# A state-space scan turned to channels on partitions, inside a fused decoder block

## The chip, the core and the metric

One core of a Trainium2 chip runs the whole block as one program. The metric is the device time of one execution in microseconds; the median of several runs counts. TensorE (PE) multiplies, VectorE (DVE), ScalarE (ACT) and GpSimd (POOL) do the elementwise work, and SyncE (SP) issues nearly all transfers.

## What is computed

One decoder layer on 512 positions of width 1024, in float32. The part that the change touches is the third mixer, a chunked state-space scan with 8 heads of 64 channels, 2 groups and a state of 128, in 4 chunks of 128 positions:

```python
xd = xh * dt[..., None]                                   # (chunk, 128, head, 64)
cs = cumsum(dt * a)                                       # within a chunk
scores = einsum("bclhn,bcshn->bclsh", ch, bh) * exp(cs_l - cs_s, lower triangle)
y_diag = einsum("bclsh,bcshp->bclhp", scores, xd)
states = einsum("bclhn,bclh,bclhp->bchpn", bh, exp(cs_end - cs), xd)
# prev: the states, carried from chunk to chunk with exp(cs_end)
y_off = einsum("bclhn,bchpn,bclh->bclhp", ch, prev, exp(cs))
y = y_diag + y_off + d_skip[:, None] * xh
y = rms_norm(y.reshape(bsz, s_len, 512) * silu(z), ssm_norm_g)
x = x + concatenate([u, att, y], axis=-1) @ w_out
```

Ahead of it stand the norm of x, the combined projection `h @ w_in` (z, x/B/C and dt are columns of it) and a causal convolution of 4 taps. Two more mixers (a convolution module and a sparse attention) fill the other columns; a second norm and a feed-forward part with 2816 hidden channels follow.

## The kernel before

The program is one list of steps, `PLAN`, built by `make_plan` (line 104). Every engine walks through the same list and does its own share of each step, so the order of the list is the order of work on each engine, and semaphores tie the engines together. The list is made of 92 slots. Each slot begins with a step `("mg", c, q)`: a quarter of the projection with weight chunk `c`, 12 matmuls of 512 columns on TensorE. A weight is split into two float32r parts (`w_hi` by ACT, line 927, `w_lo` by DVE, line 639), and so is what it is multiplied with; three products stand for one (`product`, line 1747). The other steps are placed in the slots by hand, before (`front`) or behind (`fill`) the slot's own. Chunks of weights come in this order: convolution, indexer, q, k, v, convolution, x/B/C, z, and from slot 68 on `out` for attention, convolution and scan (two halves of four slots each), then the feed-forward part in loops.

PSUM has 8 banks, in three rings that `make_groups` (line 259) lays out: `acc` (4 banks, projections), `aux` (3 banks, small products) and `out` (one bank, `pv` and `yd`). Each small product takes the next bank of its ring, and `claim` makes TensorE wait until that bank was emptied.

The scan runs beside the output projection. Chunk t begins at slot n = 68, 72, 76, 80 (`SSD_SLOTS`), with these steps:

- `csr(t)`, slot n, PE (lines 1975 to 1988): the cumulative sums as rows on top of the mask, 2 banks; then ACT (`seg`, line 1092) makes the eight blocks `dec`.
- `seg(t)`, before slot n+1, POOL (lines 880 to 885): `xd` (x times dt), `xskip` (x times d_skip) and `xdd` (`xd` times the decay to the end of the chunk). The tokens are on the partitions, 512 channels on the columns.
- `ssd(t)`, slot n+1, PE (line 1994): the products of B and C (`gt2`), then B turned (`bt`), which ACT copies (line 1101).
- `sct(t)`, before slot n+2, DVE (line 1451): scores, the product times `dec`.
- `yd(t)`, slot n+2, PE: scores as the loaded operand times `xd` moving (line 2011), `yo` (C times state, line 2019) and the new states `st` (line 2027).
- `ssdout(t)`, before slot n+3, DVE (lines 1464 to 1491): `yo` times the exponents, plus `yd`, plus `xskip`, times z, then the state.
- `ysq(t)`, slot n+3, ACT (line 1107): square with a sum over the columns; `yms(t)`, slot n+4, DVE and then POOL: the root; `yn(t)`, DVE (line 1500): times the root and the gain.
- `yT(t)`, slot n+5, PE: four blocks turned (line 1753), since the output projection wants channels on the partitions; `ssdT(t)`, before slot n+6, ACT (`ssm_hi`, line 915) and DVE (`ssm_lo`, line 1507).

The output projection adds into `x2` through DVE (`wo`, line 1563), and ends with the slots of the scan, 84 to 91. `lo` of weight chunk c is at slot 4c-3 (4c-2 for c=18), `hi` at slot 4c-4. z is projected like q, k and v, with the tokens on the partitions.

## Time and profile before

| | before |
|---|---|
| median of 3 runs | 724.64 us (724.11 to 725.85) |
| the profiled execution | 724.93 us, its span 723.2 us |
| PE busy | 698.9 us, 97% of the span |
| DVE, ACT, POOL busy | 545.2, 380.6, 141.9 us |
| granted TensorE clock, mean | 0.995 |
| matmul records | 3398 |

The page gives the busy time of each engine, the span in 40 slices, the transfers, and the chain that ended last: the path of work from the last instruction backwards, at each step to what released it. "L1747" is a line of the kernel. A fp32 matmul shows two records (two passes), a float32r matmul and a turned block one. Matmul durations are modelled and overlap each other, so times on TensorE are best taken from start to start. PEld is the load of the stationary operand.

### The profile page before, as it was taken

How to read it: one execution, taken by the hardware profiler on the slowest of the kernel's cores; microseconds unless marked ns; L12 is line 12 of the kernel's file. 1: busy time of each engine (PE TensorE's matmuls, PEld its weight loads, DVE VectorE, ACT ScalarE, POOL GpSimd, SP SyncE). 2: the span in 40 equal slices, each digit the busy share in tenths (PEclk: the TensorE clock that was granted, in tenths of full speed). 3: DMA queues.
4: the chain of work that ended last, by engine and by line, in shares of the span. 5: the costliest groups of instructions: out<-in, count | busy, mean ns of one | idle time of the engine just before them, and what ended most of it. 6: DMA issues, size and time to landing. Idle time of an engine off the chain costs nothing.

```text
span 723.2 us, 9804 instructions
## 1 busy us (share of the span) xinstructions
PE 698.9 (97%) x3398; PEld 561.2 (78%) x3402; DVE 545.2 (75%) x851; ACT 380.6 (53%) x569; POOL 141.9 (20%) x114
## 2 busy tenths in 40 slices
PE   4999999899999999999997999999999999999998
PEld 3776888667667788788796888888888888788886
DVE  5368989988998938677675777876766864887895
ACT  6354654989778675533462443343333333664651
POOL 2000468935564302233400000000000000000000
PEclk9999999999999999999998999999999999999999
DMA  8731314123021143212308887656687654864542
GB/s 248 226 126 60 117 59 116 59 61 95 21 74 46 61 179 111 87 59 60 116 2 254 240 247 231 179 178 202 196 247 231 181 164 164 290 218 136 167 164 87
DMA packets 87554, 104.09 MB, mean 144 GB/s; under 512 B 6871, under 2 KB 65591, under 8 KB 87519
## 3 DMA queue, kind: packets, MB, share of 16 engines
q1 hardware_dynamic: 87375, 103.12, 45.5%
q8 instruction: 20, 0.33, 0.2%
q10 hardware_dynamic: 144, 0.52, 0.2%
q14 instruction: 15, 0.12, 0.1%
HBM read 87.10 MB, written 16.54 MB: 143 GB/s over the span
## 4 chain that ended last, share of the span: by engine, by line
PE 81%; ACT 8%; DVE 5%; issue 3%; DMA 2%; POOL 0%; SPq 0%; POOLq 0%; DVEq 0%; ACTq 0%
PE bank L1747 70%; PE bank L1753 3%; PE bank L1767 2%; ACT w_hi L927 1%; ACT tapped L1122 1%; PE bank L1955 1%; DMA w_raw<-in_w_up 1%; DVE u_acc L621 1%; PE bank L2011 1%; PE bank L1931 1%; DVE xbcT L1415 1%; PE bank L1906 1%; ACT prob L1045 1%; DMA x_in<-in_x 1%; DVE w_lo L1584 1%
## 5 line engine op out<-in xcount | busy, mean ns | idle before, releaser
L1747 PE MATMUL bank<-h_hi,w_hi 128*128 128x512 f32 (+1 forms) x496 | 194.1, 391 | 3.7 <-DVE w_lo L1584 3.7
L1747 PE MATMUL bank<-h_lo,w_hi 128*128 128x512 f32 (+1 forms) x496 | 191.0, 385 | 0.0
L1747 PE MATMUL bank<-h_hi,w_lo 128*128 128x512 f32 (+1 forms) x496 | 190.9, 385 | 0.0
L1747 PEld LDWEIGHTS bank<-h_hi,w_hi 128*128 128x128 f32 x496 | 94.0, 189 | 29.8 <-issue 11.8
L1609 DVE SCALAR_TENSOR_TENSOR f<-bank,prm,f 128x511 f32<-128x511 f32 x88 | 65.8, 748 | 63.7 <-ACT f L1172 58.1
L1747 PEld LDWEIGHTS bank<-h_hi,w_lo 128*128 128x128 f32 x496 | 93.9, 189 | 18.5
L1747 PEld LDWEIGHTS bank<-h_lo,w_hi 128*128 128x128 f32 x496 | 93.9, 189 | 17.5
L853 POOL TENSOR_TENSOR u_acc<-tapped,u_acc 128x511 f32<-128x511 f32 (+29 forms) x60 | 90.1, 1502 | 46.2 <-ACT tapped L1122 43.0
L1172 ACT ACTIVATE f<-bank,prm 128x512 f32<-128x512 f32 x44 | 34.2, 776 | 67.6 <-PE bank L1747 67.3
L639 DVE TENSOR_TENSOR w_lo<-w_raw,w_hi 128x2048 fp32r<-128x2048 f32 x24 | 55.6, 2316 | 9.1 <-ACT w_hi L927 9.0
L1584 DVE TENSOR_TENSOR w_lo<-w_raw,w_hi 128x2048 fp32r<-128x2048 f32 x22 | 50.3, 2286 | 9.7 <-ACT w_hi L1164 9.7
L1747 PE MATMUL bank<-w_hi,g_parts 128*128 128x512 f32 x168 | 54.1, 390 | 1.1 <-DVE w_lo L1641 1.1
L1179 ACT ACTIVATE sg<-f 128x512 f32<-128x512 f32 x22 | 13.9, 632 | 74.1 <-DVE f L1609 74.1
L621 DVE SCALAR_TENSOR_TENSOR u_acc<-u_in,prm,u_acc 128x511 f32<-128x511 f32 (+29 forms) x60 | 51.9, 876 | 0.8
L1122 ACT ACTIVATE tapped<-u_in,prm 128x511 f32<-128x511 f32 (+29 forms) x60 | 40.2, 704 | 21.4 <-POOL u_acc L853 15.5
L1747 PE MATMUL bank<-w_hi,h_hi 128*128 128x512 f32 x128 | 51.2, 400 | 0.0
L1747 PE MATMUL bank<-w_hi,h_lo 128*128 128x512 f32 x128 | 50.0, 391 | 0.0
L1747 PE MATMUL bank<-w_lo,h_hi 128*128 128x512 f32 x128 | 49.9, 390 | 0.0
L927 ACT ACTIVATE w_hi<-w_raw 128x2048 fp32r<-128x2048 f32 x24 | 45.8, 1910 | 3.9 <-DMA w_raw<-in_w_in 2.5
L1164 ACT ACTIVATE w_hi<-w_raw 128x2048 fp32r<-128x2048 f32 x22 | 41.9, 1906 | 6.7 <-DMA w_raw<-in_w_up 6.7
L833 POOL TENSOR_TENSOR stats<-stats 128x1 f32<-128x1 f32 (+1 forms) x24 | 23.2, 970 | 103.1 <-DVE stats L1495 35.0
L1747 PEld LDWEIGHTS bank<-w_hi,g_parts 128*128 128x128 f32 x168 | 31.6, 188 | 8.0 <-DVE w_lo L1641 1.5
(275 smaller groups left out, 1224.7 us busy)
## 6 DMA issues: line engine op xcount, KB each, us to landing
w_raw<-in_w_up SPq DMA_DIRECT2D x44, 512.0 KB, 6.3
w_raw<-in_w_in SPq DMA_DIRECT2D x34, 512.0 KB, 4.5
down_raw<-in_w_down SPq DMA_DIRECT2D x22, 512.0 KB, 5.3
weight_sums<-down_raw SPq DMA_DIRECT2D x11, 768.0 KB, 5.2
w_raw<-in_w_out SPq DMA_DIRECT2D x12, 512.0 KB, 4.3
weight_sums<-w_sum SPq DMA_DIRECT2D x11, 512.0 KB, 2.7
w_raw<-weight_sums SPq DMA_DIRECT2D x6, 768.0 KB, 5.6
down_raw<-weight_sums SPq DMA_DIRECT2D x5, 768.0 KB, 4.4
```

The lines of the kernel that those rows point to most:

```text
L621: eng.scalar_tensor_tensor(out=u_acc[:, j, i:], in0=u_in[:, j, 0:SEQ - i], scalar=w, in1=u_acc[:, j, i:], op0=ALU.mult, op1=ALU.add).then_ ...
L639: eng.tensor_tensor(wlo[:, slot, cols], wraw[:, slot, cols], whi[:, slot, cols].bitcast(F32), ALU.subtract).then_inc(ready, 1)
L833: pool.tensor_tensor(out_, in_, half_neg[:, 0:n], ALU.pow).then_inc(ready, 1)
L853: pool.tensor_tensor(u_acc[:, j, i:], tapped[j][:, i % 4, 0:SEQ - i], u_acc[:, j, i:], ALU.add).then_inc(dw_taps[j], 1)
L927: act.activation(whi[:, c % NSLOT, :], wraw[:, c % NSLOT, :], ACT.Copy)\
L1122: act.activation(tapped[j][:, i % 4, 0:SEQ - i], u_in[:, j, 0:SEQ - i], ACT.Copy, scale=prm[:, c:c + 1]).then_inc(dwp_ready, 1)
L1164: act.activation(whi[:, c % NSLOT, :], wraw[:, c % NSLOT, :], ACT.Copy)\
L1172: act.activation(fbuf[:, 2 * s + v, :], bank[FFN_BANK[2 * s + v]][:, :], ACT.Identity, bias=prm[:, bass.ds(tile + R_FB, 1)], scale=prm[:, ...
L1584: dve.tensor_tensor(wlo[:, c % NSLOT, :], wraw[:, c % NSLOT, :], whi[:, c % NSLOT, :].bitcast(F32), ALU.subtract)\
L1609: ins = dve.scalar_tensor_tensor(out=fbuf[:, 2 * s + v, i:], in0=bank[FFN_BANK[2 * s + v]][:, 0:SEQ - i], scalar=prm[:, bass.ds(tile + (R_ ...
L1747: ins = pe.matmul(o, a, b, start=first and i == 0 and q == 0, stop=last and i == n - 1 and q == 2)
L1753: return pe.transpose(o, in_, ident[0:n, 0:n])
```

## The change

The scan's output is made with the channels on the partitions, so that it needs no turning.

- `yd`: `xd` of a head (64 columns) is loaded and the scores move (128 columns). Two heads make one block of 128 channels: the even one on the first 64 columns of the array (and partitions of the bank), the odd one on the second 64. `yo` loads a block of the state and moves C.
- The exponents exp(cs) are now wanted along the columns: a new product `eb` spreads them (8 bf16 products for t > 0, 64 columns loaded, 128 moving), ACT exponentiates into `ebc`.
- z is projected like x/B/C, weights loaded and h moving. Its loads take 256 columns of all rows in place of 512 columns of half the rows.
- `xskip` is made in four pieces of 128x128 with a scalar per partition (`dcol`, two small DVE copies of d_skip).
- The gain is a scalar per partition too, part of the parameter rows (one more `put_rows`, the transfer of `gssm` goes). ACT writes `ssm_hi` in four pieces times the gain, DVE `ssm_lo` in four.
- The norm's sum runs over partitions: ACT squares `yb`, DVE adds the four channel blocks (`yred`), TensorE sums over the partitions with a moving block of ones (`yq`), then DVE and POOL make the root `yrs`, which is a scalar per token. It is applied when the projection of the scan is added to `x2`.
- The steps: `ssdT(t)`, `yred(t)` before slot n+4, `yq(t)` in slot n+4, `yms(t)` before slot n+5; `yn` and `yT` are gone. In the `aux` ring `yq` takes the place of `yT` and `eb` is added.

```diff
+R_SG = 98
+N_ROW0 = 102
...
-        put(n + 4, ("yms", t))
-        front[n + 5].append(("yn", t))
-        put(n + 5, ("yT", t))
-        front[n + 6].append(("ssdT", t))
+        front[n + 4] += [("ssdT", t), ("yred", t)]
+        put(n + 4, ("yq", t))
+        front[n + 5].append(("yms", t))
...
-            if what in ("iq", "xbc", "conv"):
+            if what in ("iq", "xbc", "z", "conv"):
...
-            sp.dma_start(gssm[:, :], ssm_norm_g.to_broadcast([P, 512])).then_inc(s_hbc, 16)
+            put_rows(R_SG, vec(ssm_norm_g))
...
                         pool.wait_ge(ecs_ready, 1)
+                        pool.wait_ge(dcol_ready, 2)
...
-                    pool.tensor_tensor(sk3, v3, per_head(hbc[:, 2, :]), ALU.mult)\
-                        .then_inc(xd_ready, 1)
-                    pool.wait_ge(xd_ready, 3 * t + 1)
+                    for j in range(4):
+                        pool.tensor_scalar(xskip[:, P * j:P * j + P], xbcT[:, j, P * t:P * t + P],
+                                           dcol[:, j:j + 1], None, ALU.mult).then_inc(xd_ready, 1)
+                    pool.wait_ge(xd_ready, 6 * t + 1)
...
+                    if t:
+
+                        if t > 1:
+                            evacuated(act, "yo", t - 1)
+                        finished(act, "eb", t)
+                        drain(act.activation(ebc[:, :], ps("eb", t)[:, :], ACT.Exp), "eb", t)
                 elif k == "ysq":
                     t = s[1]
                     act.wait_ge(yg_ready, t + 1)
-
-                    act.activation(dump[:, :], yb[:, :], ACT.Square,
-                                   accum_out=yss[:, t:t + 1]).then_inc(yss_ready, 1)
...
+                    for j in range(4):
+                        act.activation(ssm_hi[:, j, P * t:P * t + P], yb[:, P * j:P * j + P], ACT.Copy,
+                                       scale=prm[:, R_SG + j:R_SG + j + 1]).then_inc(shi_ready, 1)
+                    if t:
+
+                        act.wait_ge(yred_ready, t)
+                    act.activation(dump[:, :], yb[:, :], ACT.Square).then_inc(ysq_ready, 1)
...
+                    for n in range(2):
+                        half = slice(SP_ * n, SP_ * n + SP_)
+                        dve.tensor_copy(dcol[half, :], hbc[half, 2, n::2]).then_inc(dcol_ready, 1)
...
+                    finished(dve, "yq", t)
+                    drain(dve.tensor_scalar(yss[:, t:t + 1], ps("yq", t)[:, 0:1], 1.0 / 512, EPS,
+                                            ALU.mult, ALU.add), "yq", t)
+                    evacuated(dve, "yq", t)
+                    dve.sem_inc(yms_ready, 1)
                 elif k == "ssdT":
                     t = s[1]
-                    wait_high(s)
+                    dve.wait_ge(shi_ready, 4 * t + 4)
                     q = slice(P * t, P * t + P)
...
+                    for j in range(4):
+                        dve.scalar_tensor_tensor(
+                            out=ssm_lo[:, j, q], in0=yb[:, P * j:P * j + P],
+                            scalar=prm[:, R_SG + j:R_SG + j + 1], in1=ssm_hi[:, j, q].bitcast(F32),
+                            op0=ALU.mult, op1=ALU.subtract).then_inc(slo_ready, 1)
+                elif k == "yred":
+                    t = s[1]
+                    dve.wait_ge(ysq_ready, t + 1)
+                    dve.tensor_reduce(ysq_sum, dump[:, :].rearrange("p (j q) -> p q j", j=4),
+                                      AX_X, ALU.add).then_inc(yred_ready, 1)
...
-                    drain(dve.tensor_tensor(xx, ps(*s)[:, :], xx, ALU.add), *s)
+                    if g == "ssm":
+
+                        dve.wait_ge(yrs_ready, t + 1)
+                        drain(dve.scalar_tensor_tensor(out=xx, in0=ps(*s)[:, :],
+                                                       scalar=yrs[:, t:t + 1], in1=xx,
+                                                       op0=ALU.mult, op1=ALU.add), *s)
...
+                    if t:
+                        claim(pe, "eb", t)
+                        for j in range(4):
+                            for n in range(2):
+                                c = SH * t + 2 * j + n
+                                ins = pe.matmul(
+                                    ps("eb", t)[SP_ * n:SP_ * n + SP_, P * j:P * j + P],
+                                    sel3[:, c:c + 1].to_broadcast([96, SP_]), cs_rows[:, :],
+                                    start=True, stop=True)
+                        ins.then_inc(aux_done, 1)
...
                     for h in range(SH):
-                        c = slice(SP_ * h, SP_ * h + SP_)
-                        ins = pe.matmul(ps("yd", t)[:, c], sct[:, h, :], xd[:, c], start=True,
+                        j, n = divmod(h, 2)
+                        ins = pe.matmul(ps("yd", t)[SP_ * n:SP_ * n + SP_, P * j:P * j + P],
+                                        xd[:, SP_ * h:SP_ * h + SP_], sct[:, h, :], start=True,
                                         stop=True)
...
-                        for g in range(SG):
-                            c = slice(256 * g, 256 * g + 256)
-                            ins = pe.matmul(ps("yo", t)[:, c], xbcT[:, 6 + g, q], state[:, c],
+                        for j in range(4):
+                            c = slice(P * j, P * j + P)
+                            ins = pe.matmul(ps("yo", t)[:, c], state[:, c], xbcT[:, 6 + j // 2, q],
                                             start=True, stop=True)
...
+                elif k == "yq":
+                    t = s[1]
+                    pe.wait_ge(yred_ready, t + 1)
+                    claim(pe, "yq", t)
+                    pe.matmul(ps("yq", t)[:, 0:32], ysq_sum, ones[:, 0:32], start=True, stop=True)\
+                        .then_inc(aux_done, 1)
```

## Rows read from the trace of the kernel before

**Rows 1.** The page: busy time of the engines, and the chain by engine.

```profile
PE 698.9 (97%) x3398; PEld 561.2 (78%) x3402; DVE 545.2 (75%) x851; ACT 380.6 (53%) x569; POOL 141.9 (20%) x114
...
PE 81%; ACT 8%; DVE 5%; issue 3%; DMA 2%; POOL 0%; SPq 0%; POOLq 0%; DVEq 0%; ACTq 0%
```

**Rows 2.** Chain in order of time, 296 to 328 us (start us, us, what).

```profile
296.05 2.18 ACT dec L1092 x8
...
311.51 0.23 PE bank L1985 x4
...
314.57 0.44 PE bank L1753 x4
315.00 0.45 PE bank L1994 x4
...
317.22 1.29 DVE sct L1451 x2
...
322.33 5.46 PE bank L1747 x24
```

**Rows 3.** Timeline of TensorE (start us, us, engine, line, operation, [idle before]).

```profile
256.12 1.10 PE L1955 MATMUL bank<-probT,v_tok 128*64 128x128 f32 x16
...
283.24 1.89 PE L2011 MATMUL bank<-xd,sct 128*128 128x64 f32 x16
...
298.27 0.20 PEld L1753 LDWEIGHTS bank<-ident,xbcT 128*128 128x128 f32 x2 [0.51 <-ACT dec L1092]
...
301.59 2.00 PE L2011 MATMUL bank<-xd,sct 128*128 128x64 f32 x16
303.43 1.08 PE L2019 MATMUL bank<-state,xbcT 128*128 128x256 f32 x4
304.34 1.03 PE L2027 MATMUL bank<-xdd,b_tok 128*128 128x256 f32 x4
...
318.55 0.41 PEld L2011 LDWEIGHTS bank<-xd,sct 128*128 128x128 f32 x3 [0.57 <-DVE sct L1451]
...
335.02 1.89 PE L2011 MATMUL bank<-xd,sct 128*128 128x64 f32 x16
```

**Rows 4.** The same view: the first mask product of chunk 2.

```profile
310.68 0.39 PE L1980 MATMUL bank<-neg_l_bf,ident_bf 128*128 128x512 bf16 x1
```

**Rows 5.** Timeline of DVE, same columns.

```profile
282.27 2.28 DVE L639 TENSOR_TENSOR w_lo<-w_raw,w_hi 128x2048 fp32r<-128x2048 f32 x1
...
304.62 0.69 DVE L1464 TENSOR_TENSOR yb<-bank,stats 128x512 f32<-128x512 f32 x1 [2.48 <-PE bank L2019]
...
309.32 0.14 DVE L1495 TENSOR_SCALAR stats<-stats 128x1 f32<-128x1 f32 x1
...
312.17 2.53 DVE L639 TENSOR_TENSOR w_lo<-w_raw,w_hi 128x2048 fp32r<-128x2048 f32 x1
```

**Rows 6.** Timeline of ACT: the square of chunk 0.

```profile
289.20 0.61 ACT L1107 ACTIVATE square_dump<-yb 128x512 f32<-128x512 f32 x1
```

**Rows 7.** Timeline of POOL: chunk 0, and chunk 2 beside a weight split.

```profile
279.95 1.04 POOL L882 TENSOR_TENSOR xskip<-xs_tok,stats 128x512 f32<-128x512 f32 x1
...
310.06 1.04 POOL L880 TENSOR_TENSOR xd<-xs_tok,stats 128x512 f32<-128x512 f32 x1
...
312.52 3.08 POOL L885 TENSOR_TENSOR xdd<-xd,stats 128x512 f32<-128x512 f32 x1
```

**Rows 8.** POOL groups by shape (busy us, mean ns, then idle before).

```profile
L616 POOL TENSOR_SCALAR u_acc<-u_in,prm 128x512 f32<-128x512 f32 x2 | 1.5, 768 | 71.0 <-DVE u_in L1318 71.0
...
L825 POOL TENSOR_SCALAR_AFFINE_SELECT neg_q<-neg_l 128x128 f32<-128x128 f32 x1 | 0.3, 293 | 0.1
```

**Rows 9.** DVE groups by shape, same columns.

```profile
L1609 DVE SCALAR_TENSOR_TENSOR f<-bank,prm,f 128x511 f32<-128x511 f32 x44 | 32.9, 747 | 58.1 <-ACT f L1172 58.1
...
L1362 DVE TENSOR_REDUCE stats<-sq 128x8 f32<-128x512 f32 x8 | 5.4, 678 | 3.4 <-ACT sq L1014 3.4
...
L1394 DVE CUSTOM_DVE_ANT_0 prob<-bank,tbias 128x128 f32<-128x128 f32 x8 | 1.9, 278 | 0.1
```

More of the change, by code:

```diff
@@ L566, in build @@
         xd_ready = sem("xd_ready")
-        yg_ready, yss_ready, yms_ready, yrs_ready, yn_ready = (
-            sem(n) for n in ("yg_ready", "yss_ready", "yms_ready", "yrs_ready", "yn_ready"))
+        yg_ready, ysq_ready, yred_ready, yms_ready, yrs_ready = (
+            sem(n) for n in ("yg_ready", "ysq_ready", "yred_ready", "yms_ready", "yrs_ready"))
+        dcol_ready, shi_ready, slo_ready = sem("dcol_ready"), sem("ssm_hi_ready"), sem("ssm_lo_ready")
         state_ready = sem("state_ready")
@@ L653, in load @@
                 done = w_landed[c % NSLOT]
-                if what in ("iq", "xbc"):
-                    c0 = C_IQ if what == "iq" else C_XBC + 256 * i
+                if what in ("iq", "xbc", "z"):
+                    c0 = {"iq": C_IQ, "xbc": C_XBC, "z": C_Z}[what] + 256 * i
                     src = w_in[:, c0:c0 + 256].rearrange("(k p) n -> p k n", p=P)
@@ L670, in load @@
                     else:
-                        c0 = {"q": C_Q, "k": C_K, "v": C_V, "z": C_Z}[what]
+                        c0 = {"q": C_Q, "k": C_K, "v": C_V}[what]
                         src = w_in[512 * i:512 * i + 512, c0:c0 + 512]
@@ L873, in _ @@
                     v3 = xs_tok[:, t, :].rearrange("p (h c) -> p h c", h=SH)
-                    x3, xx3, sk3 = (b_.rearrange("p (h c) -> p h c", h=SH)
-                                    for b_ in (xd[:, :], xdd[:, :], xskip))
+                    x3, xx3 = (b_.rearrange("p (h c) -> p h c", h=SH)
+                               for b_ in (xd[:, :], xdd[:, :]))
                     def per_head(ap):
@@ L1562, in _ @@
                     xx = x2[:, t, 512 * half:512 * half + 512]
-                    drain(dve.tensor_tensor(xx, ps(*s)[:, :], xx, ALU.add), *s)
+                    if g == "ssm":
[3 more added lines that the diff above has]
+                                                       op0=ALU.mult, op1=ALU.add), *s)
+                    else:
+                        drain(dve.tensor_tensor(xx, ps(*s)[:, :], xx, ALU.add), *s)
             dve.sem_inc(gg_ready, 1)
@@ L1863, in _ @@
                             pe.wait_ge(pool_lo_ready, POOL_LO.index(c) + 1)
-                    if what in ("iq", "xbc", "conv"):
+                    if what in ("iq", "xbc", "z", "conv"):
                         key = ("cg" if q < 2 else "ca", i) if what == "conv" else \
@@ L1880, in _ @@
                         key, k0 = ("wo", g, half, q), 0
-                        if half == 0 and g != "conv":
-                            evacuated(pe, "pv" if g == "att" else "yT", q)
+                        if half == 0 and g == "att":
+                            evacuated(pe, "pv", q)
+                        elif half == 0 and g == "ssm":
+                            pe.wait_ge(slo_ready, 4 * q + 4)
                         elif (half, q) == (0, 0):
```

65 lines of the change are left out of this document (23 added, 42 removed).

## The prediction

> **What bounds the kernel now.** I read the page first: busy times and the chain that ended last. TensorE is busy for 97% of the span, and 81% of the chain is TensorE work [rows 1]. So the time changes where TensorE's own work changes or where it is made to wait; another engine or a transfer counts only through such a wait. The second view is therefore the chain in order of time around the state-space scan (283 to 347 us), which runs between the steps of the output projection. Such a step is 12 products and takes 2.73 us (two of them 5.46 [rows 2]). I call the start of the score products of chunk t, `yd(t)`, Y(t): 283.24, 301.59, 318.55 and 335.02 [rows 3].
>
> Between Y(1) and Y(2) the chain is TensorE but for one piece: the copy of B on ACT, then `ssm_hi`, `ssm_lo`, and `sct` on DVE [rows 2]. The timeline prices that hand-over: the weights of `yd(2)` waited 0.57 us for `sct` [rows 3]. `sct` ended at 318.51 [rows 2]; without it TensorE, whose projection step ended at 318.24 by the spacing of its products, would have gone on 0.31 us earlier. At Y(1) it is 0.29, at Y(0) and Y(3) nothing. Between Y(0) and Y(1) the chain goes through ACT: the eight `dec` exponentials end at 298.23 [rows 2], and TensorE waited for them before it turned B, 0.51 us of idle weight load [rows 3]. That hand-over is set by ACT, not by TensorE.
>
> **The change part by part.** The sum is made against the profiled execution, 724.93 us (its span 723.2); the median of the runs is 0.29 lower, so I take 0.29 off at the end.
>
> *Scores move.* `yd` loads 16 score blocks (8 heads, two passes) of 128x128 and moves 64 columns past each: 1.84 us to `yo` (301.59 to 303.43 [rows 3]), 1.72 to 1.73 at t=0 and 3. Afterwards it loads 64 columns and moves 128, the two heads of a pair on two halves of the array. `pv` has exactly this form: 16 records in 1.02 us, start to next start, and 0.09 ahead of it, 1.11 [rows 3]. Gain 0.61, 0.73, 0.73, 0.62: 2.7 us. `yo` becomes four products of 128 columns for two of 256; it took 0.91 (303.43 to 304.34 [rows 3]), and four records of 128 columns take 0.45 (`gt2`, L1994 [rows 2]), so its eight take 0.90: nothing.
>
> *No turning.* Four `yT` at 0.44 (L1753 [rows 2]) go: 1.76 us. `yq` comes with two passes, each a 128x128 load and 32 columns. The 16 passes of the old `yd`, also ruled by the load, take 0.115 each, so two take 0.25 with the change-over, four `yq` 1.0 us. `ssm_hi` and `ssm_lo` leave the path into `sct`: 0.60 us gained. What is late next there is `dec`, at t=2 done some 1.3 us before `gt2`, so nothing follows at once.
>
> *Exponents along the columns (`eb`).* Eight short bf16 products for t=1..3. Four with 128 weight columns take 0.23 us (L1985 [rows 2]); halves may overlap, the change of tile size costs 0.1: between 0.23 and 0.56 a chunk, I take 0.35, nearer to `pv` since it has the same halves; 1.05 us in all. Its copy (some 0.6 us of ACT) falls where ACT has nothing to do.
>
> TensorE's own sum: -2.7 -1.76 -0.60 +1.0 +1.05 = -3.0 us.
>
> *The new wait at `yq`.* It stands one step earlier than `yT` did and needs `yred` of DVE. Queued behind it on TensorE are the mask products of the next chunk (for which ACT waits) and every projection step. From Y(1), TensorE came to the mask products after 9.09 us (301.59 to 310.68 [rows 3, 4]), now after 8.36. DVE began `ssdout` at Y+3.03 (304.62), now at Y+2.30; from there to the first instruction behind `state` and one `x` addition it is 4.70 us (309.32 [rows 5]): Y+7.00. By then ACT has made the four pieces of `ssm_hi` (`yb` is ready at Y+5.19; pieces 0.27 apart, like `dec`, 2.18 for eight [rows 2]) and the square. DVE does four pieces of `ssm_lo` (a 128-column operation takes 0.28 [rows 9], overlapped some 0.23: 0.92) and `yred` (0.68 by the one reduction in the trace [rows 9]): done at Y+8.6, seen by TensorE at Y+8.75. It waits 0.4 us at t=1 and 2. At t=3 no `state` and no `st` stand between: TensorE is there at Y+7.4, `yred` at Y+7.85, 0.45. At t=0 the turned convolution tiles hold TensorE to 292.4 while DVE is done at 291.3: nothing. Sum +1.25.
>
> *From t=0 to 1.* ACT's square with its read-out, 0.8 us from 289.20 [rows 6], becomes four pieces and a square, 1.6 us, begun 0.65 earlier because `yd(0)` is shorter. So `dec(1)` ends about when it did, at 298.4. TensorE would have been 0.45 us earlier there and would gain the 0.29 at `sct`; instead it waits at `eb(1)`, which claims the bank that `dec` empties last, then does `eb` and 12 products: Y(1)=301.7. Of TensorE's gain 0.84 us are lost here: +0.84.
>
> *Residual add.* Eight additions to `x` take a scalar: 0.75 us [rows 9] for 0.68, the price of a plain 512-column operation. Two lie on the chain through the second norm: +0.15. The root (DVE, GpSimd) moves behind another `x` addition; the last root is due two steps after `yq(3)`, so it costs nothing.
>
> *GpSimd.* Its work for chunk t+1 is queued behind the root of chunk t, which now waits for `yq(t)`: it starts 0.74 after DVE's small operation (309.32 to 310.06 [rows 5, 7]), now at Y+9.8 for Y+8.5. Then come `xd` (1.0), four skip pieces, `xdd` (1.0), and `yd` waits for the last. A skip piece is a scalar product of 128x128, which the trace lacks: between 0.29, a select of that shape, and 0.77, the scalar product with four times the columns [rows 8]. I take 0.45, nearer to its own shape. At t=0: 279.95 + 1.8 = 281.75, which is before DVE's weight split takes the port at 282.27 [rows 5, 7]; `xdd` ends at 282.8, before 283.24. Later chunks need 3.8 us and up to 2.5 in which a weight split holds GpSimd up (`xdd` beside one took 3.08 for 1.04 [rows 5, 7]): Y+16.1, and `yd(t+1)` is due at Y+16.5. Nothing, with 0.4 us of cover.
>
> The Trainium skill (SBUF — State Buffer, section "SBUF: two separate sides") calls the port that these two engines share an exclusive lock held for a whole instruction; the 3.08 us agree with it.
>
> *z, rows, copies.* z makes as many 512-column products as before, its banks are emptied at the same steps, and its loads lead their use by several steps. The gain row is a small transfer in place of a large one, and TensorE waited for neither. Two small copies on DVE lie in idle time before 264 us. Nothing, either way.
>
> Total: -3.0 +1.25 +0.84 +0.15 = -0.76 us: 724.17 for the profiled execution, **723.9** beside the median.
>
> **The rivals.**
>
> A. *The waits don't come*: DVE is in time for `yq`, and ACT's chain at t=0 shrinks as much as TensorE's work. Then all of -3.0 us stays: 721.6. For it speaks TensorE's 97%; DVE is late by only 0.4 us by my count, so that part is within reach. Against it speaks the ACT chain up to `dec(1)`. 0.17.
>
> B. *`yred` reads slowly.* It adds values that lie 512 bytes apart; the reduction in the trace reads neighbours. At twice that row, 1.36 us, t=1 to 3 lose 0.68 more each, t=0 has 1.1 of room: +2.0, 725.9. 0.25.
>
> The Trainium skill (SBUF — State Buffer, section "Door 1: The DMA port swizzle") has a rule that speaks for B: an access that goes on to a new 16-byte line pays a penalty. It gives no amount for this engine, and no row here has such a stride.
>
> C. *GpSimd becomes the bound.* The place is `xdd` ahead of `yd`. If a skip piece takes over 0.58 us, (282.27-279.95)/4, the weight split takes the port first at t=0. At 0.77: three pieces, the split until 284.55, the fourth piece and `xdd` until 286.4, for 283.24. ACT's chain moves by that less 0.65, +2.4 us. At t=2 and 3 `xdd` ends at Y+17.5, 1.0 late each. Sum +4.4: 728.3, slower. 0.12.
>
> D. *The change doesn't do what it says*: the halves of `yd` don't run beside each other, it stays at 1.8 us: +2.7, 726.6. `pv` speaks plainly against it. 0.04. The forecast keeps 0.42.
>
> **How the numbers follow.** A measurement of this kernel tells about 0.3% (2.2 us) from no change. The forecast, B and D lie within it. Faster: A, 0.17. Slower: C, and 0.03 for B or D on top of longer waits, 0.15. Same: 0.68. The range runs from A to short of C, 721.4 to 727.6; about 0.1 is left out on either side.
>
> **What would show it.** `yd` to `yo` in 1.1 us; no wait for `sct`; TensorE waiting 0.4 us for `yred` at t=1 to 3 and 0.8 for `dec` at t=1; Y(1)=301.7, then periods of 16.5 and 16.3 for 16.96 and 16.47. Against it: a `yred` of over 1 us (B); TensorE held by `xdd` (C); a wait in the second norm (355 to 372 us) that is not there now.

## The result: 1.5 us slower, and the profile after

The changed kernel takes 725.97 us (median of 13 runs, 725.69 to 727.34); the kernel before took 724.50 in 13 runs beside them (722.94 to 725.85). The ratio is 1.0024, 95% interval 1.0015 to 1.0032. The forecast was 723.9 with a range of 721.4 to 727.6: the time lies in the range, but on the other side of the kernel before. The forecast was 0.6 us faster than before, and the kernel is 1.5 us slower.

The profiled execution took 725.69 us, its span is 724.0 (before: 724.93 and 723.2). The two spans differ by less than the medians because of TensorE's clock. TensorE stands still for 3 to 4 us at 390 us, where the first weights of the up-projection are still on their way or being split, and just afterwards part of the work runs at the lower clock. How large that part is differs between executions of one kernel. By the windows view (stretch; its length; busy time of PE and its records; granted clock; DMA share; GB/s), first before, then after:

```profile
390.00:395.00 5.00, 1.46 (x4) 0.69 1.01 290
395.00:400.00 5.00, 5.00 (x16) 0.63 0.54 203
```

```profile
390.00:395.00 5.00, 1.62 (x8) 1.00 1.08 350
395.00:400.00 5.00, 4.71 (x14) 0.66 0.46 140
```

So I compare kernels in two ways: by their medians, and by the start of the first up-projection product after this gap, which I call R. In these two profiles, and in most of the others, the granted clock is 1.00 in every stretch of 5 us ahead of the gap; the three profiles where it is not are named with the experiments. The chain of waits has it, before and after (start us, us, what):

```profile
393.54 8.61 PE bank L1747 x26
```

```profile
395.29 6.73 PE bank L1773 x22
```

R moved by +1.75 us. Of this 0.20 is there from 16 us on (the input of the two executions landed 0.12 us apart, and from there to the scan the distance stays constant); 1.55 us come from the state-space scan and what follows it. Executions at equal granted clock (those of before are from the experiments) say the same: at 0.997 or 0.998 the spans of before are 722.2 to 723.0, those of after 724.0 to 724.3.

The page of after, for [rows 1]; TensorE's busy time fell by 2.4 us, and its share of the chain from 81 to 78%, in favour of ACT and DVE:

```profile
PE 696.5 (96%) x3430; PEld 556.6 (77%) x3430; DVE 548.9 (76%) x865; ACT 384.1 (53%) x580; POOL 147.4 (20%) x126
...
PE 78%; ACT 9%; DVE 7%; issue 3%; DMA 2%; POOL 0%; SPq 0%; POOLq 0%; DVEq 0%; ACTq 0%
```

The timeline of TensorE, which answers to [rows 3 and 4] (start us, us, engine, line, operation, idle before and what ended it):

```profile
283.64 1.09 PE L2049 MATMUL bank<-sct,xd 128*64 128x128 f32 x16
...
298.74 0.41 PE L2035 MATMUL bank<-cs_rows,sel 96*64 96x128 bf16 x8 [0.59 <-ACT dec L1099]
...
302.03 1.09 PE L2049 MATMUL bank<-sct,xd 128*64 128x128 f32 x16
303.05 1.16 PE L2058 MATMUL bank<-xbcT,state 128*128 128x128 f32 x8
...
304.72 0.58 PE L1773 MATMUL bank<-w_hi,att_hi 128*128 128x512 f32 x1
...
311.22 0.41 PE L2073 MATMUL bank<-ones,stats 128*128 128x32 f32 x2 [0.67 <-DVE stats L1527]
311.47 0.38 PE L2008 MATMUL bank<-neg_l_bf,ident_bf 128*128 128x512 bf16 x1
...
319.21 1.09 PE L2049 MATMUL bank<-sct,xd 128*64 128x128 f32 x16
...
328.40 0.41 PE L2073 MATMUL bank<-ones,stats 128*128 128x32 f32 x2 [0.66 <-DVE stats L1527]
...
336.20 1.09 PE L2049 MATMUL bank<-sct,xd 128*64 128x128 f32 x16
...
344.91 0.41 PE L2073 MATMUL bank<-ones,stats 128*128 128x32 f32 x2 [1.06 <-DVE stats L1527]
```

The scores are cheap as forecast: `yd` to `yo` 1.02 us for 1.84. But at every `yq` (L2073) TensorE now waits for `yred` (L1527), and the chain between Y(1) and Y(2), which was TensorE's own but for one piece, runs through DVE for almost 7 us, from 304.35 to 311.18 (chain of waits, after):

```profile
304.35 0.70 DVE yb L1481
...
305.07 0.70 DVE yb L1487
...
305.80 0.70 DVE yb L1491
...
307.13 0.70 DVE state L1500
...
308.46 0.66 DVE x L1589
...
309.32 0.87 DVE ssm_lo L1520 x3
310.19 0.99 DVE stats L1527
...
311.22 0.41 PE bank L2073 x2
```

The starts of `yd` in a table (us; "forecast" is the text on record; 0.20 is taken off the times of after, the shift from the start):

| | before | after, less 0.20 | step before | step after | step forecast |
|---|---|---|---|---|---|
| Y(0) | 283.24 | 283.44 | | | |
| Y(1) | 301.59 | 301.83 | 18.35 | 18.39 | 18.5 |
| Y(2) | 318.55 | 319.01 | 16.96 | 17.18 | 16.5 |
| Y(3) | 335.02 | 336.00 | 16.47 | 16.99 | 16.3 |
| R | 393.54 | 395.09 | 58.52 | 59.09 | 58.3 |

### The profile page after: what moved, and what is told of

The parts are those of the page before. It is cut to its first block, busy times and chain, and to the rows that moved or that the text cites. A ratio compares the mean times of both kernels' runs of the same rounds, so it can differ in the third digit from the quotient of the medians.

```text
span 724.0 us, 9909 instructions
## 1 busy us (share of the span) xinstructions
PE 696.5 (96%) x3430; PEld 556.6 (77%) x3430; DVE 548.9 (76%) x865; ACT 384.1 (53%) x580; POOL 147.4 (20%) x126
## 4 chain that ended last, share of the span: by engine, by line
PE 78%; ACT 9%; DVE 7%; issue 3%; DMA 2%; POOL 0%; SPq 0%; POOLq 0%; DVEq 0%; ACTq 0%
PE bank L1773 68%; PE bank L1779 3%; PE bank L1793 2%; ACT w_hi L934 1%; ACT tapped L1134 1%; PE bank L1983 1%; DVE u_acc L626 1%; DMA w_raw<-in_w_up 1%; PE bank L1959 1%; DVE xbcT L1429 1%; PE bank L1934 1%; DMA x_in<-in_x 1%; ACT prob L1052 1%; DVE w_lo L1610 1%; PE bank L2049 1%
## 5 line engine op out<-in xcount | busy, mean ns | idle before, releaser
L1773 PE MATMUL bank<-h_hi,w_hi 128*128 128x512 f32 (+1 forms) x528 | 206.9, 392 | 3.7 <-DVE w_lo L1610 3.7
L1773 PE MATMUL bank<-h_hi,w_lo 128*128 128x512 f32 (+1 forms) x528 | 202.9, 384 | 0.0
L1773 PE MATMUL bank<-h_lo,w_hi 128*128 128x512 f32 (+1 forms) x528 | 202.8, 384 | 0.0
L1773 PEld LDWEIGHTS bank<-h_hi,w_hi 128*128 128x128 f32 x528 | 99.6, 189 | 31.6 <-issue 12.8
L1773 PEld LDWEIGHTS bank<-h_hi,w_lo 128*128 128x128 f32 x528 | 99.5, 188 | 20.1
L1773 PEld LDWEIGHTS bank<-h_lo,w_hi 128*128 128x128 f32 x528 | 99.7, 189 | 18.3
L644 DVE TENSOR_TENSOR w_lo<-w_raw,w_hi 128x2048 fp32r<-128x2048 f32 x24 | 58.1, 2423 | 8.5 <-ACT w_hi L934 8.4
L1610 DVE TENSOR_TENSOR w_lo<-w_raw,w_hi 128x2048 fp32r<-128x2048 f32 x22 | 50.3, 2287 | 9.6 <-ACT w_hi L1178 9.6
L1773 PE MATMUL bank<-w_hi,h_hi 128*128 128x512 f32 x96 | 38.0, 395 | 0.0
L1773 PE MATMUL bank<-w_hi,h_lo 128*128 128x512 f32 x96 | 37.4, 390 | 0.0
L1773 PE MATMUL bank<-w_lo,h_hi 128*128 128x512 f32 x96 | 37.4, 389 | 0.0
```

Of the source, the lines that this page charges most:

```text
L644: eng.tensor_tensor(wlo[:, slot, cols], wraw[:, slot, cols], whi[:, slot, cols].bitcast(F32), ALU.subtract).then_inc(ready, 1)
L1610: dve.tensor_tensor(wlo[:, c % NSLOT, :], wraw[:, c % NSLOT, :], whi[:, c % NSLOT, :].bitcast(F32), ALU.subtract)\
L1773: ins = pe.matmul(o, a, b, start=first and i == 0 and q == 0, stop=last and i == n - 1 and q == 2)
```

## The experiments

All kernels but one start from the changed kernel and change what each diff shows. Each was run beside the kernel before (medians of 724.33 to 724.50). "R" is from the profiled run. Two things in these profiles are not the edit's, and the last column takes them off:

- The port at t=0 (column "port", experiment 8). Where the weight split got it ahead of `xdd(0)`, TensorE waits 2.17 us at `yd(0)`.
- TensorE's clock after a wait. In `x2_pesum` and `x6_root` the granted clock is 0.67 and 0.66 from 285 to 290 us, behind that same wait (0.50 from 287 to 289); in `x3_order` and `x8_apart` it is 1.00 there. From Y(0) to the next projection product it is 4.46 and 4.41 us for 2.78, from Y(0) to Y(1) 19.78 and 20.03 for 18.39, so 1.4 and 1.6 are taken off (an estimate: that the step would be the changed kernel's at full clock). In `y2_before_late` the clock is 0.66 from 305 to 310, and 1.7 are taken off (experiment 7).

The windows view, `x3_order` and then `x6_root`, same columns as above but with all engines (PE, PEld, DVE, ACT, POOL):

```profile
285.00:290.00 5.00, 4.27 (x35) 3.73 (x36) 2.75 (x5) 1.61 (x3) 0.63 (x1) 1.00 0.59 210
```

```profile
285.00:290.00 5.00, 4.39 (x28) 3.62 (x29) 2.32 (x4) 0.13 (x1) 1.35 (x2) 0.66 0.64 210
```

| kernel | median us | to before, 95% | R | port at t=0 | R, port and clock off |
|---|---|---|---|---|---|
| before | 724.4 | | 393.54 | | 393.54 |
| after | 725.97 | 1.0015 to 1.0032 | 395.29 | `xdd` | 395.29 |
| `x3_order` | 724.76 | 1.0002 to 1.0020 | 396.01 | split | 393.84 |
| `x1_near` | 725.28 | 1.0004 to 1.0022 | 394.76 | `xdd` | 394.76 |
| `x2_pesum` | 727.76 | 1.0025 to 1.0050 | 397.57 | split | 394.0 |
| `x5_skip1` | 725.74 | 1.0011 to 1.0029 | 395.22 | not met | 395.22 |
| `x9_order_skip1` | 722.82 | 0.9968 to 0.9986 | 392.17 | not met | 392.17 |
| `x6_root` | 729.63 | 1.0057 to 1.0081 | 399.33 | split | 395.5 |
| `x8_apart` | 729.85 | 1.0066 to 1.0095 | 399.34 | split | 397.17 |
| `z3_late` | 727.30 | 1.0031 to 1.0065 | 394.05 | `xdd` | 394.05 |
| `y2_before_late` | 727.21 | 1.0030 to 1.0059 | 396.84 | | 395.1 |
| `y1_x9_late` | 721.49 | 0.9953 to 0.9978 | 390.63 | not met | 390.63 |
| `z1_lo18` | 727.94 | 1.0044 to 1.0073 | 395.51 | `xdd` | 395.51 |

**1. Is it the wait for `yred`?** `x3_order` makes it due earlier: ACT squares before it writes the gain pieces, DVE reduces before it writes `ssm_lo`.

```diff
-                    for j in range(4):
-                        act.activation(ssm_hi[:, j, P * t:P * t + P], yb[:, P * j:P * j + P], ...)
                     if t:
                         act.wait_ge(yred_ready, t)
                     act.activation(dump[:, :], yb[:, :], ACT.Square).then_inc(ysq_ready, 1)
+                    for j in range(4):
+                        act.activation(ssm_hi[:, j, P * t:P * t + P], yb[:, P * j:P * j + P], ...)
...
-                    front[n + 4] += [("ssdT", t), ("yred", t)]
+                    front[n + 4] += [("yred", t), ("ssdT", t)]
```

> The changed kernel, with the square ahead of the four gain pieces on ScalarE, and yred ahead of the four ssm_lo pieces on VectorE; nothing else. Theory T (the loss is TensorE waiting for yred): yred then ends at about Y+8.1, before TensorE reaches yq at Y+8.4, and the waits of 0.8, 0.8 and 1.1 us at t=1, 2, 3 go: 2.7 us less, 723.3 where the changed kernel has 726.0. Rival G (GpSimd is next): xdd ends at Y+16.8 whatever VectorE does, yd(t+1) would be due at Y+16.3, so only 0.3 us each remain of the first two waits and all of the third: 1.7 us less, 724.3, and the trace shows TensorE waiting for xdd. Rival S (the loss is TensorE's own work, changes of tile size and the added products): no change.

724.76 us, 1.2 less than the changed kernel; R without the lost port 1.45 less. None of the three waits for `yred` is left. They had cost 2.9 us (0.84, 0.83 and 1.2, worked out below), so about half came back; this profile shows where the rest went, as the expectation's rival G had it (with 1.7 us gained for 1.2):

```profile
285.73 1.09 PE L2049 MATMUL bank<-sct,xd 128*64 128x128 f32 x16 [2.17 <-issue]
...
321.18 1.09 PE L2049 MATMUL bank<-sct,xd 128*64 128x128 f32 x16 [0.74 <-issue]
...
338.24 1.09 PE L2049 MATMUL bank<-sct,xd 128*64 128x128 f32 x16 [0.96 <-issue]
```

At t=2 and 3 TensorE comes earlier to `yd` and waits there instead. The view names no releaser, but GpSimd's timeline of the same run has `xdd` end at 321.08 and 338.13, each just ahead of `yd`:

```profile
320.04 1.04 POOL L892 TENSOR_TENSOR xdd<-xd,stats 128x512 f32<-128x512 f32 x1
...
337.09 1.04 POOL L892 TENSOR_TENSOR xdd<-xd,stats 128x512 f32<-128x512 f32 x1
```

So GpSimd stood right behind DVE as the next bound, with the 0.4 us of cover that the prediction gave it at t=2 gone.

**2. Is it how `yred` reads?** `x1_near` lets ACT write the squares interleaved, so that the four values of a sum are neighbours.

```diff
-                    act.activation(dump[:, :], yb[:, :], ACT.Square).then_inc(ysq_ready, 1)
+                    act.activation(dump[:, :].rearrange("p (q j) -> p j q", j=4),
+                                   yb[:, :].rearrange("p (j q) -> p j q", j=4),
+                                   ACT.Square).then_inc(ysq_ready, 1)
...
-                    dve.tensor_reduce(ysq_sum, dump[:, :].rearrange("p (j q) -> p q j", j=4),
+                    dve.tensor_reduce(ysq_sum, dump[:, :].rearrange("p (q j) -> p q j", j=4),
```

> The changed kernel, where ScalarE writes the squares interleaved (the four channel blocks of a position next to each other), so that yred reads neighbours; the same 128 sums of 4. yred took 1.06 us where the reduction in the trace of before took 0.68. If the stride of its reads is the reason: 0.68 here, TensorE waits 0.38 less three times, 1.1 us less in all, 724.9; ScalarE's square may take longer for its strided writes, which hides as long as it stays under 1.3 us. If the number of results (128 for 8) is the reason: yred stays at 1.06, no change.

DVE's and ACT's timelines, first after, then `x1_near`:

```profile
309.06 1.13 DVE L1520 SCALAR_TENSOR_TENSOR ssm_lo<-yb,prm,ssm_hi 128x128 fp32r<-128x128 f32 x4
310.11 1.06 DVE L1527 TENSOR_REDUCE stats<-square_dump 128x128 f32<-128x512 f32 x1
...
308.44 0.62 ACT L1125 ACTIVATE square_dump<-yb 128x512 f32<-128x512 f32 x1
```

```profile
310.75 0.68 DVE L1529 TENSOR_REDUCE stats<-square_dump 128x128 f32<-128x512 f32 x1
...
309.08 1.11 ACT L1125 ACTIVATE square_dump<-yb 128x512 f32<-128x512 f32 x1
...
299.39 0.41 PE L2037 MATMUL bank<-cs_rows,sel 96*64 96x128 bf16 x8 [0.59 <-ACT dec L1099]
...
311.49 0.41 PE L2075 MATMUL bank<-ones,stats 128*128 128x32 f32 x2 [0.28 <-DVE stats L1529]
```

The same reduction over neighbours takes 0.68 us, over values 512 bytes apart 1.06. The waits at `yq` fall to 0.28, 0.28 and 0.7. But ACT pays for the strided writing (1.11 for 0.62), and at t=0 that lengthens the chain to `dec(1)`: Y(1) is 302.67, with its start 0.28 later than after's. Net 725.28, 0.7 less, where the expectation had 1.1 less. The stride costs 0.38 us of DVE a chunk, 1.1 in three; the rest of the wait has other causes.

**3. Must DVE make the sum at all?** `x2_pesum` leaves the reduction out; TensorE sums the four blocks itself and waits only for ACT's square.

```diff
-                    pe.wait_ge(yred_ready, t + 1)
+                    pe.wait_ge(ysq_ready, t + 1)
                     claim(pe, "yq", t)
-                    pe.matmul(ps("yq", t)[:, 0:32], ysq_sum, ones[:, 0:32], start=True, stop=True)\
-                        .then_inc(aux_done, 1)
+                    for j in range(4):
+                        ins = pe.matmul(ps("yq", t)[:, 0:32], dump[:, P * j:P * j + P],
+                                        ones[:, 0:32], start=j == 0, stop=j == 3)
+                    ins.then_inc(aux_done, 1)
```

> The changed kernel without yred: TensorE adds the four channel blocks itself, four products of one block of squares with ones in place of one; it waits for ScalarE's square. Theory T: the waits for yred (0.8, 0.8, 1.1 us) go, 24 more passes of 0.12 us come, 2.9 us: 726.0 +0.2, and the waits at yq are under 0.2 us. GpSimd's xdd at Y+16.8 may hold part back: TensorE reaches yd(t+1) at about Y+17.1, so no. Rival S (TensorE's own work doesn't count fully): 724 or less.

The waits are gone, and `yq` takes 0.81 us to the next start, for 0.14 to 0.25. Its median is 1.8 us above the changed kernel's, but its profiled run lost the port at t=0 and had the lower clock behind it. From Y(1), where both are over, to R it takes 92.11 us for 93.26, 1.15 less; with port and clock off, R is 1.3 less. Its other runs agree: at a granted clock of 0.997 their spans are 725.0 and 725.1, for 724.0 to 724.2 in the changed kernel, which is the port's 2.17 less some 1.2 (that they lost the port is inferred, as in experiment 8). So moving the sum to TensorE gains nearly what `x3_order` does (1.4 us from Y(1) to R), more than its expectation had (0.2 lost).

**4. Is it GpSimd?** `x5_skip1` makes the skip term with one product of 128x512 for four of 128x128; `x9_order_skip1` does so on top of `x3_order`.

```diff
-                    for j in range(4):
-                        pool.tensor_scalar(xskip[:, P * j:P * j + P], xbcT[:, j, P * t:P * t + P],
-                                           dcol[:, j:j + 1], None, ALU.mult).then_inc(xd_ready, 1)
+                    pool.tensor_tensor(xskip.rearrange("p (j q) -> p j q", j=4),
+                                       xbcT[:, 0:4, P * t:P * t + P],
+                                       dcol.unsqueeze(2).to_broadcast([P, 4, P]),
+                                       ALU.mult).then_inc(xd_ready, 1)
```

> The changed kernel with xskip made by one GpSimd product of 512 columns in place of four of 128; VectorE's order as in the changed kernel. T: nothing on the path moves, within 0.3 us of the changed kernel (xdd was ready 0.1 to 0.7 us before yd at each chunk). If GpSimd already held TensorE up in the changed kernel: 1 us or more less. In either case the weight split on VectorE, 3.0 us where it lies beside GpSimd, falls to 2.3 to 2.6.

> As x3_order, and xskip made by one GpSimd product of 512 columns (the scalar of each partition and block spread along the positions) in place of four of 128. T without G: as x3_order, the single product changes nothing. G: the single product takes 1.0 us for 2.35, and no longer lies under the weight split, xdd ends 1.3 to 3 us sooner, and the part of x3_order's gain that was kept back comes: 723.3, 1.0 below x3_order.

Alone it gives nothing (725.74 for 725.97; R 395.22 for 395.29): while TensorE waits for `yred`, `xdd` is in time. Once that wait is gone, the same edit gives 1.9 us more (724.76 to 722.82; R 393.84 to 392.17), and no wait at `yd` is left. The two bounds lie one behind the other, and only their removal together makes the change faster than the kernel before. GpSimd's timeline of `x9_order_skip1`:

```profile
280.39 1.05 POOL L888 TENSOR_TENSOR xskip<-xbcT,stats 128x512 f32<-128x512 f32 x1
281.39 1.05 POOL L893 TENSOR_TENSOR xdd<-xd,stats 128x512 f32<-128x512 f32 x1
...
313.67 3.09 POOL L888 TENSOR_TENSOR xskip<-xbcT,stats 128x512 f32<-128x512 f32 x1
316.72 1.04 POOL L893 TENSOR_TENSOR xdd<-xd,stats 128x512 f32<-128x512 f32 x1
```

**5. Is it the root's place?** GpSimd's products for chunk t+1 are queued behind the root of chunk t. `x6_root` puts the root behind them.

```diff
-        front[n + 5].append(("yms", t))
+        put(n + 5, ("yms", t))
```

> The changed kernel with the root of chunk t placed behind GpSimd's products of chunk t+1 (one list position later), so that GpSimd no longer waits for yq ahead of them. They then begin at about Y+5.2 instead of Y+9.9 and xdd is ready by Y+11. Theory T: xdd was in time in the changed kernel, so this gains nothing, and since these products now lie beside VectorE's state and ssm_lo operations, which take the same port, yred comes later: 0 to 1 us more in each of t=1 to 2, 726 to 728. If GpSimd was on the path: 1 us less.

R is 4.0 us above the changed kernel's, but 2.17 of it are the port at t=0 and 1.6 the clock behind that wait; the edit's own part is the 0.25 and 0.19 us by which the steps to Y(2) and Y(3) are longer (17.43 for 17.18, 17.18 for 16.99), within the 0 to 1 us that was expected of each. The products now start when `yb` is ready and run beside DVE's `state` and `ssm_lo`, and the four pieces of `ssm_lo` take 1.38 us for 1.13, so `yred` is later still:

```profile
312.67 1.38 DVE L1520 SCALAR_TENSOR_TENSOR ssm_lo<-yb,prm,ssm_hi 128x128 fp32r<-128x128 f32 x4
313.97 1.06 DVE L1527 TENSOR_REDUCE stats<-square_dump 128x128 f32<-128x512 f32 x1
...
315.08 0.41 PE L2073 MATMUL bank<-ones,stats 128*128 128x32 f32 x2 [0.91 <-DVE stats L1527]
```

**6. Do the halves of `yd` run beside each other?** `x8_apart` takes the four even heads and then the four odd ones, so that neighbours in the order use the same half.

```diff
-                    for h in range(SH):
+                    for h in (0, 2, 4, 6, 1, 3, 5, 7):
```

> The changed kernel, where yd goes through the four even heads and then the four odd ones, so that neighbouring passes use the same half of the array; same products, same results. The changed kernel's yd takes 1.02 us from its first pass to the next product, which I ascribe to the two halves running beside each other. Then each of the 16 passes stands alone here, 0.11 us, yd takes 1.8 us as before the change: 0.8 us more each, 3.1 us in all, 729. If instead the shorter load (64 columns) is what made yd quick, it stays at 1.0 and the time at 726.

```profile
304.65 1.58 PE L2049 MATMUL bank<-sct,xd 128*64 128x128 f32 x16
306.17 1.16 PE L2058 MATMUL bank<-xbcT,state 128*128 128x128 f32 x8
```

The same 16 passes take 1.52 us for 1.02 to the start of `yo`; the step Y(1) to Y(2) is 17.66 for 17.18. By R, port off, 1.9 us, four times 0.5. The expectation of 0.8 each was too high: passes on one half cost 0.095 each here, not the 0.115 that [rows 3] show for the full width. So of the 0.82 us by which `yd` became shorter, 0.5 are the two halves beside each other, and 0.32 the form of the products (64 columns loaded, 128 moving) alone.

**7. The chain from t=0 to 1.** `z3_late` puts both halves of weight chunk 19 one slot later, so that ACT's table load need not wait for `w_hi`; `y1_x9_late` does so on top of `x9_order_skip1`, `y2_before_late` in the kernel before.

```diff
-        fill[4 * c - 4].append(("hi", c))
-        fill[4 * c - (2 if c == LATE_LO else 3 if c < UP0 else 4)].append(("lo", c))
+        d = c == 19
+        fill[4 * c - 4 + d].append(("hi", c))
+        fill[4 * c - (2 if c == LATE_LO else 3 if c < UP0 else 4) + d].append(("lo", c))
```

> The changed kernel with the halves of weight chunk 19 (ACT's w_hi of 1.9 us, which runs at 293.3 us ahead of the table load and dec(1), and VectorE's w_lo) one slot later, and nothing else. Theory (my term t=0 to 1: ACT's chain sets Y(1)): the table load starts as soon as the mask products are done, dec(1) ends some 1.0 us or more earlier, the waits of TensorE for dec at the turning of B (0.39 us) and at eb(1) (0.59 us) go, Y(1)-Y(0) falls from 18.39 to 17.5 or less, 725.0 us. Rival: TensorE's own work and the hand-over of sct set it, and the later weight halves make another step wait: 725.7 to 726.5.

> The kernel before with the halves of weight chunk 19 one slot later, and nothing else. It tells how much of what that move gives was there to be had without the change. Theory: in the kernel before TensorE waited for dec(1) only once (0.51 us of idle weight load, some 0.3 us of TensorE), since the four products that turned y and the products behind them gave ACT time; so it gives 0.3 to 0.6 us here, 723.9 to 724.2, against 0.9 us or more in the changed kernel. Rival: the wait is worth the same in both (the ACT chain sets both): 723.3 to 723.6.

> x9_order_skip1 with hi of weight chunk 19 placed behind the exponents of chunk 1 of the scan, and its lo behind sct(1) (both one slot later). Theory A (between Y(0) and Y(1) ScalarE's chain sets the time: four pieces, square, turned tiles, weight split, table load, dec): dec(1) ends 1.9 us earlier, the waits of TensorE for it (0.4 and 0.6 us) go, Y(1) comes 1.0 us sooner and the time falls by 1.0, to 721.8. Rival: the weight chunk is then late at slot 76, or GpSimd or yred is next, and the gain stays under 0.3 us.

In `z3_late` the table load starts at 293.72 for 295.22, both waits for `dec` are gone, Y(1) is 300.74 for 302.03, and R is 394.05 for 395.29, 1.24 us less, 0.2 to 0.3 more than expected. The median shows nothing of it: 727.30. The profiled run pays it back to the clock (a granted clock of 0.81 and 0.51 from 390 to 400 us for 1.00 and 0.66 in after), and the other five runs are 0.7 to 3.6 us above the profiled one; two of them have a span of 726.4 at its own granted clock of 0.995, where it has 724.0, and by their clock all five are long enough to have lost the port (experiment 8). On `x9_order_skip1` the median does fall, from 722.82 to 721.49, and R by 1.54.

In the kernel before the same edit costs 3.3 us at R, 2.9 in the median, where 0.3 to 0.6 were to be gained: a miss, and the expectation had not looked at what stands behind the split. TensorE's, DVE's and ACT's rows of `y2_before_late`:

```profile
303.08 2.00 PE L2012 MATMUL bank<-xd,sct 128*128 128x64 f32 x16 [1.91 <-DVE sct L1452]
...
301.14 0.69 DVE L1508 TENSOR_TENSOR ssm_lo<-bank,ssm_hi 128x512 fp32r<-128x512 f32 x1 [5.04 <-ACT ssm_hi L916]
301.74 1.28 DVE L1452 TENSOR_TENSOR sct<-bank,dec 128x512 f32<-128x512 f32 x2
...
298.71 1.91 ACT L928 ACTIVATE w_hi<-w_raw 128x2048 fp32r<-128x2048 f32 x1
300.51 0.59 ACT L916 ACTIVATE ssm_hi<-bank 128x512 fp32r<-128x512 f32 x1
```

The split stands ahead of `ssm_hi`, behind which `ssm_lo` and `sct` are queued. In the changed kernel no `ssm_hi` and no `ssm_lo` stand in that place. Y(1) is 1.2 us later by it (0.27 of shift from the start taken off). After this wait TensorE's granted clock is 0.66 from 305 to 310 us, which is 1.7 us of work at full clock, as much as Y(3) falls behind Y(1) more (35.11 for 33.43).

**8. The port at t=0.** The weight split and `xdd(0)` reach the port that DVE and GpSimd share at 282.47 and 282.49 in the profile of after. `z1_lo18` was meant to part them by one slot of the schedule.

```diff
-        fill[4 * c - (2 if c == LATE_LO else 3 if c < UP0 else 4)].append(("lo", c))
+        fill[4 * c - (2 if c in (LATE_LO, 18) else 3 if c < UP0 else 4)].append(("lo", c))
```

> The changed kernel with one thing moved: VectorE's weight split number 18, which reaches the shared port at 282.47 us in its trace, 0.02 us ahead of GpSimd's xdd(0) at 282.49, stands one slot later (some 0.7 us or more). Theory: who gets the port at t=0 is open in the changed kernel, and where the split wins TensorE waits some 2.2 us at yd(0). With the split later xdd(0) is always first: Y(0) without a wait, xdd about 1.05 us, no run of this kernel 1 us or more above its fastest ones, the median 0 to 0.5 us below that of the changed kernel (725.5 to 726.0). Rival: the spread of the runs comes from elsewhere (the kernel before has one of 1.5 us too, without this meeting); then the runs spread as before, 725.7 to 727.3, and the median is the same. If the split now meets the first addition of yb(0) or the state, ssm_lo(0) ends later, which costs nothing at yq(0).

The edit changes nothing: `LATE_LO` (line 91) is itself 18, so the condition gives the same list of steps. The kernel is a repetition of the changed one. Its profiled run is the changed kernel's (Y(0) 283.84, R 395.51, each 0.2 later, periods equal), but the five other runs do not fit: spans of 726.1 to 726.3 at a granted clock of 0.997 or 0.998, where the changed kernel has 724.0 to 724.3, and 727.4 to 727.7 at 0.995. They are 2.1 us longer at the same clock. Four profiles show what is of that size: in `x3_order`, `x2_pesum`, `x6_root` and `x8_apart` TensorE waits 2.17 us at `yd(0)`, because the split got the port. DVE's and GpSimd's rows, after and then `x3_order`:

```profile
282.47 3.21 DVE L644 TENSOR_TENSOR w_lo<-w_raw,w_hi 128x2048 fp32r<-128x2048 f32 x1
...
282.49 1.05 POOL L892 TENSOR_TENSOR xdd<-xd,stats 128x512 f32<-128x512 f32 x1
```

```profile
282.45 2.28 DVE L644 TENSOR_TENSOR w_lo<-w_raw,w_hi 128x2048 fp32r<-128x2048 f32 x1
...
282.50 3.13 POOL L892 TENSOR_TENSOR xdd<-xd,stats 128x512 f32<-128x512 f32 x1
```

One of the two pays for the other, and TensorE waits 2.17 us for `xdd` in the second case. None of the 13 runs of the changed kernel is long enough for its clock to have lost, none of 11 of `x1_near`, one of 11 of `x3_order`, five of six of `z1_lo18` and of `z3_late`, and all 20 of `x2_pesum`, `x6_root` and `x8_apart`. That the unprofiled runs lost the port is an inference from their length; the profiled ones show it. So the medians of these five contain some 2.1 us that are not the edit's. What decides between the two orders from run to run stays open. Where `xdd(0)` ends before the split comes (`x5_skip1`, `x9_order_skip1`, `y1_x9_late`), no run of 27 has the long form.

## Why the prediction was wrong

The step that failed is *the new wait at `yq`*: 1.25 us stood in the sum, 2.9 are in the profile. That is 1.65 of the 2.3 us between the forecast (0.76 less) and what R shows (1.55 more), and enough to turn the sign. The mechanism was the forecast's own, TensorE waiting for `yred`; its size was not. Of the rest most is `eb` and the hand-over of `sct`. Nearly all terms that were off were off in one direction.

*Scores move, no turning.* Right: 1.02 us and 0.09 ahead of it, for 1.84; the turn products are gone; first projection product behind `yo` and `st` 2.69 us after Y(1) for 3.43, a gain of 0.74 against 0.73. D is refuted (experiment 6).

*`yo` at nothing.* Eight products of 128 columns took 1.00, not 0.90: +0.1 each at t=1 to 3. It is within the 0.74, because the 0.09 of the change of tile size lay ahead of Y and not behind it.

*The hand-over of `sct`.* Gone as forecast, but the forecast counted all of its 0.31 us at t=2. Projection step to `yd(2)` takes 2.97 us for 3.13, a gain of 0.16: the 12 products with the change to half-width tiles ahead of `yd` take 0.15 more than their own 2.82.

*`eb`.* From the turning of B to the projection step it is 0.66 us for 0.13, so +0.53 for a forecast 0.35, which lies near the upper end that was kept (0.56). Eight products take 0.34 from start to start, and tile sizes change on both sides of them.

*The wait at `yq`* was 0.84 (311.22 less the 310.38 at which TensorE's steps would have ended), 0.83 and, by the same count, 1.2 (344.91 less 343.69), where 0.4, 0.4 and 0.45 stood. DVE's start (Y+2.32 for 2.30) and the start of `ssm_lo` (Y+7.03 for 7.00) were right. Then `ssm_lo` took 1.05 to the next start for 0.92, and `yred` 1.06 for 0.68. `x1_near` shows the stride to be the cause of that 0.38. At t=3 `ssm_lo` stood 0.75 us still for ACT's last piece (pieces 0.30 apart, not 0.27) and began at Y+6.54, where the forecast's Y+7.85 leaves Y+6.1 for it. In sum 2.9 for 1.25: +1.65.

*t=0 to 1.* Right, as a hand-over set by ACT: `dec(1)` ended at 298.48 less the shift for a forecast 298.4, and Y(1) came at 301.83 for 301.7. Experiment 7 shows that ACT sets it.

*Residual add.* Right: 0.74 us each; from the start of a weight split of ACT's at 352.05 (353.70 after) to R the distance grows by 0.10 for 0.15.

*GpSimd.* A skip piece takes 0.58 us from start to start, 2.35 for four, not 0.45, which is just the value that rival C named as its deciding point. Beside a weight split four take 4.38, and `xdd` ends 0.67, 0.29 and 0.10 us before `yd(t)` for t=1 to 3. So C was not the cause of the difference, but it was nearer than its 0.12: it happens by the hundredth of a microsecond at t=0 (+2.1, experiment 8), and it is what the removal of the `yred` wait runs into (experiment 1).

The budget of Y(1) to Y(2), forecast and measured: -0.48 and +0.22. The difference of 0.70 is 0.44 at the wait, 0.18 at `eb`, 0.15 at `sct`, less 0.07 in small pieces. Over the scan: 0.13 up to Y(1), 0.68, 0.69, and 0.8 behind Y(3), nearly all of it the longer wait (1.2 for 0.45).

*The rivals.* B was the nearest in its cause and in its time (725.9 for 725.97), but right for half its reason: it priced `yred` at 1.36 and 2.0 us in all, measured are 1.06 and 1.1. The same sum was filled by the pieces of ACT and DVE, by `eb` and by the tile changes, so that its time agrees to 0.1 us is luck. The Trainium skill (SBUF — State Buffer, section "Door 1: The DMA port swizzle") speaks of a penalty for an access that goes on to a new 16-byte line; the 1.06 for 0.68 agree, and the price is that of these traces. A's three microseconds were there to be had: `x9_order_skip1` has 1.6 of them, with both waits removed, and `y1_x9_late` 2.9 (724.38 to 721.49, ratio 0.9953 to 0.9978), the fastest kernel of all.

*The chances.* "Slower by over 0.3%" did not come either (0.24%); the sign did. The fault is in how the terms were rounded: where one engine was to be 0.4 us late, each unknown on its way (a stride, the pitch of 128-column pieces, an order of ACT) could only make it later, and I took for each the nearest row and not the nearest row with such an access.

## What to carry to other kernels

When TensorE's work is moved to an engine that stands one step ahead of it, price the moved operations with the stride and the size that they will have, and expect waits to add up while TensorE's savings are used only up to the next late engine. Look for the second bound at the same time: here neither the later `yred` nor the four GpSimd pieces were worth removing alone (1.2 and 0.2 us), together 3.1. A change that takes an operation off an engine's queue can be worth more by the freedom it gives than by itself: a weight split moved by one slot made Y(1) 1.2 us later before the change and 1.3 us earlier after it. And before a median is put down to an edit, look whether its profile lost time where the edit isn't: here a meeting at the port (2.17 us) and the clock behind it (1.4 to 1.6 us) were larger than most edits.

## What the runs showed of the hardware

- A reduction on DVE of 128x512 fp32 values in groups of four takes 0.68 us over neighbours and 1.06 at a distance of 512 bytes; on ACT a square of the same size takes 0.62 us written in order and 1.11 written at a distance of 16 bytes.
- On GpSimd four `tensor_scalar` of 128x128 take 2.35 us, one `tensor_tensor` of 128x512 takes 1.05.
- Of two instructions that reached the shared port 0.01 to 0.05 us apart, the one that lost took 3.13 for 1.04 (`xdd`), or 3.21 for 2.28 (the split). The Trainium skill (SBUF — State Buffer, section "SBUF: two separate sides") calls it a lock for a whole instruction, which agrees. In all eight profiles with the meeting the split's record starts first: by 0.04 or 0.05 us in the four where it got the port, by 0.01 or 0.02 in the four where it lost it. By their lengths (an inference) runs of one program went both ways.
- 16 fp32 passes of 64 weight columns and 128 moving ones take 1.02 us alternating between the halves of the array and 1.52 with eight on one half and then eight on the other. Going over to another tile size left PEld idle for 0.17 to 0.35 us, of which 0.1 to 0.2 reach TensorE's products.
- After an idle stretch of 1.9 us in the scan (`y2_before_late`) TensorE's granted clock was 0.66 over the next 5 us. After one of 2.17 us at `yd(0)` it was 0.67 and 0.66 from 285 to 290 us in two profiles (`x2_pesum`, `x6_root`) and 1.00 in two others (`x3_order`, `x8_apart`). After the gap of over 3 us at 390 us it was 0.63 in one execution and 1.00 in another (`y1_x9_late`).
